# Two attention norms turned unscaled, and one matmul for both halves of the up projection's operand

## The reference, cut to what matters

```
# first block, second half
n = modulate(rmsnorm(h, norm_g1), shift, scale)
z = dwconv(n @ w_up, conv_w, conv_b)          # 2048 x 11264, 3 taps over the tokens
g, v = split(z); h = h + m5 * ((silu(g) * v) @ w_down)   # 5632 x 2048
x = rmsnorm(h, final_g)                       # end of the first block
# second block: 16 meta tokens ahead of x, L = 272
a = rms_norm(x, a_norm) @ w_in                # q, k, v, gate: 2048 x 8192
x = x + (subln(diff_attention(rope(q), rope(k), v)) * silu(gate)) @ w_out
k, v = split(rms_norm(x, kv_norm) @ w_kv)     # 2048 x 512
q, gate = split(rms_norm(x, b_norm) @ b_w_in) # 2048 x 4096
x = x + (attention_with_sinks(rope(q), rope(k), v) * silu(gate)) @ b_w_out
out = rms_norm(x, final_norm)[:, 16:]
```

## Time and profile before

| | us |
|---|---|
| median of 3 runs | 2506.17 (2499.54 to 2509.42) |
| profiled execution | 2499.73 |
| its span | 2498.0 |
| TensorE busy | 2315.4 |
| VectorE busy | 1563.9 |
| ScalarE busy | 1109.2 |

### The profile page before, as it was taken

One profiled execution on the slowest core, in us unless ns is written; L12 is line 12 of the kernel. 1 busy time (PEld: TensorE's weight loads), 2 busy tenths in 40 slices (PEclk: granted clock), 3 DMA queues, 4 the chain that ended last, 5 costly groups with the idle time before them and its releaser, 6 DMA issues.

```text
span 2498.0 us, 38136 instructions
## 1 busy us (share of the span) xinstructions
PE 2315.4 (93%) x14675; PEld 2082.5 (83%) x14675; DVE 1563.9 (63%) x1879; ACT 1109.2 (44%) x1674; POOL 116.5 (5%) x213
## 2 busy tenths in 40 slices
PE   1399999999899999999999979999999998999997
PEld 1388888887699988999899869988988997768786
DVE  7766677777568865666555646656556544566754
ACT  0254444443364443444344544444444444445543
POOL 0001100011001100000000000000000000000000
PEclk9699999999999999999999989999999998999999
DMA  9888888688658855545655634434443543533353
GB/s 402 320 277 294 279 263 276 228 315 306 207 186 282 302 183 193 186 166 193 196 186 179 210 101 155 150 119 135 134 134 119 169 161 99 161 118 102 106 188 112
DMA packets 219331, 492.87 MB, mean 197 GB/s; under 512 B 9331, under 2 KB 12057, under 8 KB 214073
## 3 DMA queue, kind: packets, MB, share of 16 engines
q1 hardware_dynamic: 195280, 415.27, 48.7%
q0 software_dynamic: 18752, 67.71, 8.2%
q10 hardware_dynamic: 5178, 8.19, 1.0%
HBM read 488.48 MB, written 2.10 MB: 196 GB/s over the span
## 4 chain that ended last, share of the span: by engine, by line
PE 81%; DVE 9%; DMA 4%; ACT 3%; issue 2%; DVEq 0%; POOL 0%; POOLq 0%; ACTq 0%; SPq 0%
PE ps L1488 37%; PE ps L1470 32%; DMA ada<-in_ada_w 3%; PE ps L1855 2%; PE ps L1505 2%; DVE acc L953 2%; DVE wlo L897 2%; DMA rawv<-in_ada_w 1%; ACT whi L448 1%; PE ps L1717 1%; PE ps L1825 1%; ACT eb__123 L822 1%; DVE acc L906 1%; PE ps L1817 1%; PE ps L1571 1%
## 5 line engine op out<-in xcount | busy, mean ns | idle before, releaser
L897 DVE TENSOR_TENSOR wlo<-raw,whi 128x1024 fp32r<-128x1024 f32 x720 | 873.5, 1223 | 627.5 <-ACT whi L448 625.5
L448 ACT ACTIVATE whi<-raw 128x1024 fp32r<-128x1024 f32 x720 | 756.1, 1058 | 877.8 <-PE ps L1470 429.7
L1488 PE MATMUL ps<-xth,whi 128*128 128x256 f32 x1408 | 400.3, 284 | 2.6 <-DVE wlo L897 1.8
L1488 PE MATMUL ps<-xtl,whi 128*128 128x256 f32 x1408 | 399.2, 284 | 0.0
L1488 PE MATMUL ps<-xth,wlo 128*128 128x256 f32 x1408 | 399.1, 283 | 0.0
L1488 PE MATMUL ps<-xmh,whi 128*128 128x272 f32 x1088 | 324.2, 298 | 0.0
L1488 PE MATMUL ps<-xmh,wlo 128*128 128x272 f32 x1088 | 316.4, 291 | 0.0
L1488 PE MATMUL ps<-xml,whi 128*128 128x272 f32 x1088 | 315.1, 290 | 0.0
L1488 PEld LDWEIGHTS ps<-xth,whi 128*128 128x128 f32 x1408 | 271.1, 193 | 3.7 <-DVE wlo L897 2.0
L1488 PEld LDWEIGHTS ps<-xtl,whi 128*128 128x128 f32 x1408 | 271.1, 193 | 0.1
L1488 PEld LDWEIGHTS ps<-xth,wlo 128*128 128x128 f32 x1408 | 271.1, 193 | 0.0
(11 more groups left out here) (250 smaller groups left out, 3605.0 us busy)
## 6 DMA issues: line engine op xcount, KB each, us to landing
raw<-in_a_w_in SPq DMA_DIRECT2D x128, 1024.0 KB, 5.4
raw<-in_ffn_w_up SPq DMA_DIRECT2D x88, 1024.0 KB, 5.1
ada<-in_ada_w POOLq DMA_DIRECT2D x128, 512.0 KB, 4.8
raw<-in_a_w_out SPq DMA_DIRECT2D x48, 1024.0 KB, 5.3
raw<-in_ffn_w_down SPq DMA_DIRECT2D x44, 1024.0 KB, 5.1
rawv<-in_ada_w SPq DMA_DIRECT2D x32, 1024.0 KB, 7.2
raw<-in_b_w_in SPq DMA_DIRECT2D x32, 1024.0 KB, 5.4
raw<-in_b_w_out SPq DMA_DIRECT2D x16, 1024.0 KB, 5.0
```

Source lines behind the costliest of these rows:

```text
L448: act.activation(whi[:, r % 4], raw[:, r // 2, r % 2], ACT.Copy).then_inc(hi_ready, 1)
L897: dve.tensor_tensor(wlo[:, r % 4], raw[:, r // 2, r % 2], whi[:, r % 4].bitcast(F32), ALU.subtract).then_inc(lo_ready, 1)
L1488: mm = pe.matmul(ps[:, bank + c, 0:n_tok], ws[w], x[:, 2 * r + i, 0:n_tok], start=first and i == 0 and n == 0, stop=last and i == 1 and n ...
```

## The change

- **Up projection.** `xt_` puts `xth` and `xtl` into one tile, so that one matmul takes the high weights against the high and the low half of a k-tile: 512 columns, one PSUM bank, high in columns 0 to 255 and low in 256 to 511. A second one adds the low weights against the high half. ScalarE copies the second halves of four banks (`low_out`), VectorE adds the first halves (`summed`), and the taps read that tile (`gs`, `vs`) in SBUF. TensorE waits for `gs_ready` and `vs_ready`.
- **Norm "a".** `h` is turned by plain transposes, 12 of the 16 tiles between the units of the last down projection, 4 between those of the heads stage (`A_TURN_AT`). The product of the first block's final gain and the norm's gain (`again`) is applied on the way out of PSUM. The factor per token goes onto the results: into the scale of the scores for q, onto k and the gate by a row of factors `rb_a` (VectorE now reads those banks: `scaled_out`), and into the copy of v. Sums, masks and the small tables of the stage become steps beside units (`a_setup`).
- **Norm "b".** Each 512 columns of `h` are added, squared and turned while the next output chunk runs (`Y_TURN_AT`, `B_TURN_AT`, `B_IN_AT`); the tiles take no gain. The gains of keys and queries go onto the weights (`cast_gained`, `lo_gained`, 72 units), the factor onto the results (`pair_out`'s scale, the tables of the rope, `rb_b` for the gates). Queries and gates use `xmh`/`xml` too, and their operands skip the meta tokens (`token_cols`). The rope of the keys moves from step 4 to step 7.

```diff
+A_TURN_AT = [6 * n + 8 + i for n in range(4) for i in range(4)]
+Y_TURN_AT = (11, 19, 27, 33)
+B_TURN_AT = (13, 21, 29, 35)
+def token_cols(x, c0):
+    return x[:, c0:c0 + 2 * (P + NM)].rearrange("p (b q) -> p b q", q=P + NM)[:, :, 0:P]
...
+        xt_ = place("xt_", [P, 2, KT * L], O_XT, F32R)
+        xth, xtl = (xt_[:, i, 0:KT * T].rearrange("p (k q) -> p k q", q=T) for i in range(2))
...
+            def cast_gained(G, r, gain):
...
+                for i in range(2):
+                    c = act.activation(whi[:, r % 4, i], raw[:, r // 2, r % 2, i], ACT.Copy,
+                                       scale=gain[:, 2 * r + i:2 * r + i + 1])
+            def low_out(x, bank, lsem):
+                act.activation(x[:, :, :], ps[:, bank:bank + 4, T:2 * T], ACT.Copy).then_inc(sem(lsem), 1)
+            def lo_gained(G, r, gain):
...
+                for i in range(2):
+                    low = dve.scalar_tensor_tensor(out=wlo[:, r % 4, i], in0=raw[:, r // 2, r % 2, i],
+                                                   scalar=gain[:, 2 * r + i:2 * r + i + 1],
+                                                   in1=whi[:, r % 4, i].bitcast(F32), op0=ALU.mult, op1=ALU.subtract)
+            def summed(x, bank, lsem, F, done):
+                dve.wait_ge(sem(lsem), F + 1)
+                dve.tensor_tensor(x[:, :, :], x[:, :, :], ps[:, bank:bank + 4, 0:T], ALU.add).then_inc(sem(done), 1)
...
                         if t == 3 and not first:
+                            summed(vs, 4, "vs_low", F - 1, "vs_ready")
+                        if t == 4 and not first:
                             value_done(F - 1)
-                        if t == 6 and not first:
+                        if t == 7 and not first:
                             h_lo(F - 1, f - 1)
                         if t == 11:
-                            side_taps(yg, 0, F * 4, "yg_ready", F, "yg_done")
+                            summed(gs, 0, "gs_low", F, "gs_ready")
+                        if t == 12:
+                            side_taps(yg, gs, F * 4, "yg_ready", F, "yg_done")
...
+            def scaled_out(n, G, dst):
...
+                    dve.tensor_tensor(dst[:, c, :], ps[:, c, 0:L], rb_a[:, :], ALU.mult).then_inc(sem("bank_read"), 1)
...
+            def up_unit(G, r, bank, first, last, resid=None):
...
+                    both = ps[:, bank + c, :].rearrange("p (b q) -> p b q", q=T)
+                    for i in range(2):
+                        k = 2 * r + i
+                        pe.matmul(both, whi[:, r % 4, i, c * P:c * P + P], xt_[:, :, k * T:k * T + T],
+                                  start=first and i == 0, stop=last and i == 1, skip_group_check=True)
+                        mm = pe.matmul(ps[:, bank + c, 0:T], wlo[:, r % 4, i, c * P:c * P + P], xth[:, k, :],
+                                       start=False, stop=last and i == 1, skip_group_check=True)
...
+            def turned_a(t):
+                if t in A_TURN_AT:
+                    k = A_TURN_AT.index(t)
+                    pe.wait_ge(sem("resid_f"), 18 + k // 4 * 2)
+                    if k >= 3:
+                        pe.wait_ge(sem("nl"), TILES0["a"] + k - 2)
+                    for src, c0 in ((h[:, 0], 0), (h[:, 1], P + NM)):
+                        mm = pe.transpose(ps[:, 4 + k % 3, c0:c0 + P], src[:, k * P:k * P + P], ident[:, :])
...
             for t in range(8 * nf):
...
+                    if p == 2:
+                        turned_a(t)
                     tok_unit(*at(gd, t), hth, htl, 2 * r, 2 * (n % 2), r == 0, r == 2 * nf - 1)
-            pe.wait_ge(sem("gained"), 4)
-            pe.wait_ge(sem("meta_loaded"), 16)
-            for k in range(4):
-                turned_tile("a", k)
...
-            pe.wait_ge(sem("y_added"), 12)
-            for k in range(4):
-                turned_tile("b", k)
```

More of the change, by code:

```diff
@@ L641, in pair @@
                             value_out(F - 1)
-                        if t == 5 and not first:
+                        if t == 4 and not first:
+                            value_taps(F - 1)
+                        if t == 6 and not first:
                             h_out(F - 1, f - 1)
@@ L772, in gate_out @@
             def gate_out(g):
-                banks_out(12 + g, G_GATE + g + 1, ACT.Tanh, gth, "gth_ready")
+                for c in range(4):
+                    act.wait_ge(sem("bank_read"), (12 + g) * 4 + (c + 1))
+                    act.activation(gth[:, c, :], g2[:, c, :], ACT.Tanh, scale=0.5).then_inc(sem("gth_ready"), 1)
             def oth_out(g):
@@ L865, in _ @@
                     else:
[L866 removed]
+                        gate_out(n - 4)
                 quad_act(t)
@@ L1423, in _ @@
             for t in range(72):
-                spread("b", t + 8, b_dests)
-                if t == 4:
+                if t == 2:
+                    diagonals("b", ((52, P), (53, NM), (54, P)))
+                if t == 5:
+                    token_factors()
+                if t == 7:
                     rope_k()
@@ L1437, in _ @@
                     quad_dve(t)
-                if n >= 4 and t % 8 == 3:
+                if n >= 4 and t % 8 == 4:
+                    gb_silu(n - 4)
                     gb_times(n - 4)
@@ L1654, in pair @@
                     else:
-                        pe.wait_ge(sem("yg_done"), F)
+                        pe.wait_ge(sem("gs_ready"), F)
                     for r in range(8):
@@ L1676, in _ @@
                     if r == 0 and n < 2:
-                        pe.wait_ge(sem("yg_done"), f0 + nf)
+                        pe.wait_ge(sem("gs_ready"), f0 + nf)
                     elif r == 0:
@@ new lines, in spread_factors, with kv_turn @@
+            def spread_factors():
+                pe.wait_ge(sem("dg"), DG_AT["b"])
+                for d, (c0, w) in enumerate(BLK):
+                    mm = pe.matmul(ps[:, 7, c0:c0 + w], ones[0:w, :], dg[0:w, d, 0:w], start=True, stop=True)
+                mm.then_inc(sem("rb_spread"), 1)
+            def kv_turn():
+                pe.wait_ge(sem("kk_raw"), 1)
+                pe.wait_ge(sem("tabB_loaded"), 32)
+                for i in range(2):
+                    mm = pe.matmul(ps[:, 2 + i, 0:L], rotB[:, :], kk[:, i, :], start=True, stop=True)
+                mm.then_inc(sem("rotb"), 1)
+                pe.wait_ge(sem("dve_own_b"), 5)
+                for b, (c0, w) in enumerate(BLK):
+                    bank, col = ((6, 0), (6, 256), (7, 0))[b]
+                    for i in range(2):
+                        mm = pe.transpose(ps[0:w, bank, col + i * P:col + i * P + P], kk[:, 2 + i, c0:c0 + w], ident[:, :])
+                mm.then_inc(sem("vb_turned"), 1)
```

503 lines of the change are left out of this document (313 added, 190 removed).

## The result

The changed kernel takes 2466.1 us (median of four; 2465.8 to 2471.1), the kernel before 2507.8 us (2499.5 to 2509.4) on the same chip: ratio 0.9848, interval 0.9831 to 0.9866. The gain is about 42 us where the forecast had 64. The profiled execution took 2466.2 us for a span of 2464.5.

The account below looks back on a forecast made before the run. TensorE, busy 93% of the span, was taken as the bound. Terms -18.6 + 4.5 - 27.7 - 25.4 + 1.5 + 2 = -63.7 us took 2499.7 to 2436.0; with 6.4 for the runs' median, 2442, range 2426 to 2472.

Parts of the forecast that it names:

- First norm: Attention norm between last down projection and heads: 34.4 us lost before, 6.7 added back, net -27.7 us.
- Second norm: Attention norm between output product and B stage: 34.6 us lost before, 9.2 added, net -25.4 us.
- Joined matmul: Up projection on TensorE: 0.106 us less in each of 176 units by joining two 256-column matmuls, -18.6 us.
- Part 0: Up projection's part 0: VectorE, also adding `ada` rows, stalls TensorE 0.4 us in one pair, 2 in two; +4.5 us.
- B stage: Two-part casts' extra 0.41 us fits VectorE's 1.14 us wait for scores; +1.5 us; forecast wrong if B grows over 8.
- Heads: Heads stage: VectorE instead of ScalarE reads K banks and does a second pass for the gates; +2 us.
- first rival: VectorE and ScalarE make the waits in B and heads, both upper bounds: +24.5 us, 2467; chance 0.13.
- second's: Second rival: joining saves little, a joined matmul takes 0.240 us; 18.6 us less gain, 2461; chance 0.10.

Follow-up runs that it names:

- e1_three: Changed kernel with the joined matmul undone: three matmuls of 256 columns for each k-tile and channel group; 2475.5 us, ratio 0.9873.
- e2_nosum: Changed kernel with VectorE's sum after each up chunk cut to one column, low-half products left out of the result; 2465.6 us, ratio 0.9841.
- e4_ada: Changed kernel with VectorE's ten `ada` adds in part 0's loop spread to other steps; 2463.6 us, ratio 0.9826.
- e5_plain: Changed kernel with plain one-instruction casts for the 72 units of keys, values and B, norms' gains left out; 2458.7 us, ratio 0.9813.
- e9_ratio: Changed kernel with B's gain back on the turned tiles, KV weights scaled by the gains' quotient, B's casts plain; 2461.7 us, ratio 0.9818.
- after: First profile of the changed kernel itself, nothing altered; profiled execution 2466.2 us, span 2464.5.
- c0_again: Changed kernel run and profiled a second time, unchanged; 2465.6 us, ratio 0.9835.

## Why the prediction was right and where it was off

The time lies inside the prediction's range, 24 us above the value named. In part that is luck: the range reached so far up for B and heads alone, and half of what is missing came from the joined matmul and part 0. By its steps:

- **First norm, -27.7: right** (-29.0). The 12 tiles between down units cost 0.22 us each, as the 0.11 a transpose had it; no wait of TensorE over 0.5 us is left there, and the clock is 1.00.
- **Second norm, -25.4: right.** -25.1 in its own stretch against -28.0. The 3 us are the turned tiles of B: four groups of 12 transposes were priced by a row of 12 in 1.32 us, and the chain has them at 2.12 (L1985), while the output's own turn (L1971) stays at 1.31:
```profile
2051.35 1.31 PE ps L1971 x12
...
2058.73 2.12 PE ps L1985 x12
2060.85 15.11 PE ps L1650 x120
```
  Again a duration taken from another sequence of the same instruction.
- **Joined matmul, -18.6: mechanism right, size half.** The term was 1408 times 0.2267 + 0.1200; measured was 0.3533 a pair in parts 1 and 2, so -9.3 (e1_three). The durations were taken from runs of equal matmuls; taking turns, a pair ran at their sum only in stretches of part 0.
- **Part 0, +4.5: right in kind, short in size.** Parts 1 and 2 gained 3.3 and 2.5 us, part 0 gained 3.4 by the joining and still came out 3.9 us longer (195.1 against 191.2, means of two): +7.3. The forecast had the place of the long stop right (the third `ada` step), but took 0.4 to 2 us a pair. TensorE's waits in part 0 were 7.8 and 5.8 us in the two profiles (the longest 5.3 and 2.7) against 1.8 and 0.6 before, and 3.8 and 3.4 us at half clock against 2.0 and none. Taking VectorE's sum away brought 5 to 7 us back, 3.4 to 4.9 of them at full clock (e2_nosum); spreading the adds did not (e4_ada).
- **B stage, +1.5: wrong, and this is the step that the text itself had named as what would make it wrong** (growth by over 8). "The extra 0.41 us of the casts before the scores fits into the 1.14": it did not. It is 0.64 us (0.37 and 0.27), and the slack was read off one quad and one engine. In the quad before that one, with a rope, VectorE has no such slack. It is itself the chain, and the low weights of two units stand in it between `rb` and the masked scores `sb`; one of the two in the kernel before, then in the changed one:
```profile
2184.93 1.22 DVE wlo L897
2186.16 1.21 DVE sb__122 L1365
```
```profile
2140.93 1.42 DVE wlo L983 x2
2142.34 1.21 DVE sb__123 L1508
```
  From `rb` to `sb` it takes 6.6 us there instead of 6.2. The `ob` and `wtb` waits grew by 2.2 and 3.1 us. The casts account for about 4 us at full clock (e5_plain, e9_ratio), other parts of the change for 4.6. Of these, 2.6 were priced under the norm, and which part made the other 2 stays open. The clock adds 4.3 (9.4 against 5.1, means of two).
- **Heads, +2: right at full clock** (+1.8). The remaining 3.4 us are half-clock stretches, which differ from one execution to the next: twelve profiles of kernels of the changed form lost 8.5 to 17.1 us in this stage (mean 13.8), the two of the kernel before 5.1 and 10.3. Without them the stage, from its first unit, takes 476.6 to 478.3 us in all twelve. No term of the sum had this, though the earlier trace rows showed the clock at 0.99 and not 1.00. Whether the changed form loses more on average, or twelve against two is chance, stays open; its stops there have nearly the same number and lengths (24.9 us in 17 stops against 25.9 in 18).

So of the 25 us that are missing between the means of the profiles (22 between the medians), the joined matmul explains 9.3, part 0 about 3, B at full clock 4.5, the half-clock stretches in B and heads about 8; the two norms took 1.6 more together, and all else gave 1 back. The time is that of the first rival (2467), but its cause is half the second's: the forecast held the two for alternatives, and both came in part.

## What to carry to other kernels

A term that multiplies a small duration by a thousand needs the duration from the same sequence of instructions, not from rows of each kind by itself; where no such row exists, halve the gain or widen the range by it. Slack of an engine in one place doesn't hide work that is added to every step: ask for the longest chain over a whole repeat (here a quad of B), on both engines. And read the granted clock of more than one profile before a difference of a few us in a stage is put down to a change.

## What the hardware showed

- A pair of a 512- and a 256-column matmul in this type goes at 0.3467 or at 0.3533 us, steadily, and changes only where TensorE paused (0.15 us was enough in e2_nosum); a block of eight and eight goes at 0.230 and 0.119. Why it settles on one of the two wasn't found.
- In the heads, a stop of TensorE of 1 to 2.4 us was sometimes followed by a stretch at 1.2 GHz that cost 1.7 or 3.4 us: six times in the changed kernel's first profile and three times in its second, of 17 and 18 stops. The same stops in the same kernel were followed by it in one execution and not in another (after: at 1567 and 1609; c0_again: neither).
- ScalarE's 128x512 copy with a scale from memory took 713 ns, VectorE's 128x512 multiply and subtract with a factor per partition 748 ns, against 692 for a plain add of that size (L1138).
